# Gather matmuls of the next expert pair moved into the waits of an expert's first overflow block

## The chip, the core and the metric

The kernel runs on one NeuronCore of a Trainium2 chip. The metric is the device time of one execution in microseconds (us). Engines are named as in the profile: PE is the matmul engine (PEld its weight loads), ACT the scalar engine, DVE the vector engine, POOL the GpSimd engine, SP the engine that issues most DMAs. ACTq and SPq are DMAs that ACT and SP issue; an issue keeps its engine's instruction stream for the time shown.

## What is computed

The reference runs a two-layer trunk over 384 tokens (128 of a prompt and 256 samples) of width 1024. A layer is a token mixer (differential attention, then retention) and a mixture of 16 experts, in which each token uses two. Only the expert part matters here:

```python
s = sigmoid(t @ w_router)                    # t: 384 x 1024
gates = top-2 of 16 inside the best of 4 groups, normalised
for wg, wu, wd, ge in experts:               # wg, wu: 1024 x 512, wd: 512 x 1024
    a = silu(t @ wg) * (t @ wu) * ge[:, None]
    y = y + a @ wd
```

All of it is in float32. Which expert a token takes is known only on the chip.

## The kernel before

Both layers call `experts(l)` once on each engine; each engine has a program of its own, and semaphores order them. The 16 experts run in eight pairs. For an expert `e` (`x` is its place in the pair), PE does this:

- gate and up products of the first 64 tokens routed to the expert, lines 1089 and 1090, 8 rounds, into PSUM bank `x`;
- `overflow(e, ...)`: tokens beyond 64 are done in blocks of 32. The numbers of blocks are cumulated on the chip in a table `RT[l]`, so that an expert's blocks run from `RT[l][e]` to `RT[l][e + 1]`. PE loads both into registers (lines 998 and 999), and if they are equal it jumps over the block's code; else it loops over the blocks (`Fori`). A block gathers 32 tokens (line 1014, semaphore `o_gathered`), waits for DVE's copy (`o_rows`), transposes (1025), waits for DVE (`o_xs`), does gate and up (1031), waits for ACT's silu and DVE's product (`o_gated`), transposes (1037), waits for DVE (`o_aT`) and does the down product (1043);
- three quarters of a gather, line 986: nine products that pick, by a 0/1 matrix `sel`, the tokens of the same place in the next pair, into PSUM bank `2 + x`. It needs `sel` and `xs`, which come from the pair before;
- four transposes, line 1103, which need `gated` and signal `T`; then the last quarter of the gather (three products), then the down products, lines 1120 and 1121, which need `aT`.

A float32 product is two MATMUL records (and two weight loads) in the trace, so nine products are "x18"; a transpose is one.

ACT does for each expert: silu (line 1463), the overflow loop, and the copy that gives `aT` (line 1466, after `T`), then the copy of a finished gather half (1434). For experts before 14 the overflow loop on ACT is a silu (1442), a wait for `o_y`, and then four DMA issues that store the block's rows (line 1450). They stand ahead of line 1466 in ACT's stream:

```python
act.wait_ge(m["o_y"], o + 1)
for j in range(4):
    act.dma_start(scratch[ds(o * OVB + LAST * BLK, OVB), QC * j:QC * j + QC],
                  oy[OVB * j:OVB * j + OVB, :]).then_inc(m["o_stored"], 16)
```

`o_y` is signalled by DVE's copy of the down result (line 1935), which waits for line 1043. SP loads weights into a ring of slots: a gate or up slot is loaded again after `T` of its old expert, a down slot after `down` (line 603).

Experts 14 and 15 (`LAST` is 14) have no next pair, so no gather.

Of the kernel before, what the change touches and what calls it, by code (L numbers as in the profile page):

```python
# [16 lines left out]
P = 128  # L17
# [6 lines left out]
DEPTH = 2  # L24
# [210 lines left out]
def trunk_kernel(nc, ins, outs, scratch):  # L235
# [31 lines left out]
    with ctx:  # L267
# [30 lines left out]
        RT = [sb(f"route_tab{l}", [1, NE + 1], I32) for l in range(DEPTH)]  # L298
# [337 lines left out]
        def _(pe):  # L636
# [322 lines left out]
            def experts(l):  # L959
# [20 lines left out]

                def gather(half, kts):

                    for kt in kts:
                        out = psum[:, 2 + half, P * (kt % 4):P * (kt % 4) + P]
                        for t in range(TT):
                            last = mm(out, htok[:, t, P * kt:P * kt + P], sel[:, t].rearrange("p x s -> p (x s)"),  # L986
                                      start=t == 0, stop=t == TT - 1)
                    return last
# [7 lines left out]
                def overflow(e, wg, wu, hint):  # L996
# [3 lines left out]
                    ov = psum[:, 7, :]  # L1000
                    with unless_equal(pe, f"pe_blocks_{l}_{e}", lo, hi, hint):
# [8 lines left out]
                        with pe.Fori(lo, hi) as o:  # L1010
                            pe.wait_ge(m["o_sel"], o + e + 1)
                            for t in range(TT):
                                for j in range(4):
                                    last = mm(ov[OVB * j:OVB * j + OVB, 0:QC], osel[:, t, :], htok[:, t, QC * j:QC * j + QC],
                                              start=t == 0, stop=t == TT - 1)
                            last.then_inc(m["o_gathered"], 1)
                            if e >= LAST:
                                for t in range(TT):
                                    last = tr(psum[:, 4, P * t:P * t + P], oselw[:, t].rearrange("p n s -> p (n s)"), ident)
                                last.then_inc(m["o_selT"], 1)  # L1020
                            else:
                                pe.sem_inc(m["o_selT"], 1)
                            pe.wait_ge(m["o_rows"], o + 1)
                            for k in range(2):
                                last = tr(ov[:, QC + P * k:QC + P * k + P], osg[:, P * k:P * k + P], ident)
                            last.then_inc(m["o_turned"], 1)
                            pe.wait_ge(m["o_xs"], o + 1)
                            for kt in range(KT):
                                for j in range(4):
                                    w = (wg, wu)[j // 2]  # L1030
                                    last = mm(ov[OVB * j:OVB * j + OVB, 0:QC], ox[:, kt, :], w[kt][:, QC * (j % 2):QC * (j % 2) + QC],  # L1031
                                              start=kt == 0, stop=kt == KT - 1)
                            last.then_inc(m["o_gu"], 1)
                            pe.wait_ge(m["o_gated"], o + 1)
                            settle(pe, l)
                            for k in range(2):
                                last = tr(ov[:, BLK * k:BLK * k + BLK], oa[0:BLK, P * k:P * k + P], ident[0:BLK, 0:BLK])
                            last.then_inc(m["o_T"], 1)
                            pe.wait_ge(m["o_aT"], o + 1)
                            for k in range(4):  # L1040
                                a = oaT[:, k % 2, OVB * (k // 2):OVB * (k // 2) + OVB]
                                for j in range(4):
                                    last = mm(ov[OVB * j:OVB * j + OVB, 0:QC], a, wd[k][:, QC * j:QC * j + QC], start=k == 0, stop=k == 3)
# [1162 lines left out]
```

## Time and profile before

| | us |
|---|---|
| median of three runs | 1444.04 (1442.41 to 1446.9) |
| the profiled execution | 1440.93 |
| its span, first to last instruction | 1439.0 |
| PE busy | 1354.5 (94%) |
| DVE busy | 517.8 (36%) |
| ACT busy | 282.2 (20%) |
| mean granted PE clock | 0.983 of full speed |

The profile is of one execution. A row of a timeline has the start and the duration in us, the engine, the line, the operation, output and inputs, the count, and in brackets the idle time of that engine ahead of it with what ended it. Ends of matmuls are modelled. "issue" is idle time for which the profile shows no releaser. The expert part takes about 340 to 600 us in layer 0 and 1113 to 1410 us in layer 1.

### The profile page before, as it was taken

What the parts mean: (1) busy time and instruction counts of PE and PEld (TensorE: products, weight loads), DVE (VectorE), ACT (ScalarE), POOL (GpSimd) and SP (SyncE); (2) the same over time, 40 slices, a digit from 0 to 9 for tenths busy, and PEclk for the clock granted to TensorE, in tenths of its full rate; (3) what the DMA queues carried; (4) which work ended last, traced back from release to release, by engine and by line L of the source; (5) the groups of instructions that cost most, each with busy time, mean ns of one, the idle gap of its engine ahead of it and who ended that gap; (6) DMA issues with size and microseconds to landing.
All of it is one profiled execution on the core that took longest, in us unless ns stands there. A gap on an engine that the chain in (4) does not pass through costs nothing.

```text
span 1439.0 us, 17852 instructions
## 1 busy us (share of the span) xinstructions
PE 1354.5 (94%) x6816; PEld 768.3 (53%) x6816; DVE 517.8 (36%) x1376; ACT 282.2 (20%) x580; POOL 47.2 (3%) x63
## 2 busy tenths in 40 slices
PE   5899999997998999889999999999998998899997
PEld 2456556555444444447667567576565544444434
DVE  3145355625111111554464653744513311111123
ACT  3143344411010111231120221212111100001013
POOL 1001200000000000100000000100100000000010
PEclk9999999998999999999999999999999899999998
DMA  9967686926999999912323423224534799579891
GB/s 363 322 244 231 224 279 237 380 95 238 392 396 350 398 395 378 388 64 94 117 82 117 146 88 110 95 89 139 182 118 174 254 398 387 190 258 398 324 399 52
DMA packets 162742, 344.83 MB, mean 240 GB/s; under 512 B 5929, under 2 KB 23554, under 8 KB 162626
## 3 DMA queue, kind: packets, MB, share of 16 engines
q1 hardware_dynamic: 150320, 319.19, 60.4%
q10 hardware_dynamic: 9362, 14.37, 2.7%
q0 software_dynamic: 2944, 9.65, 2.5%
q8 instruction: 82, 1.34, 0.4%
q14 instruction: 34, 0.28, 0.1%
HBM read 324.96 MB, written 18.22 MB: 238 GB/s over the span
## 4 chain that ended last, share of the span: by engine, by line
PE 85%; DMA 6%; DVE 4%; ACT 2%; SPq 2%; issue 1%; DVEq 0%; ACTq 0%
PE psum L1089 14%; PE psum L771 11%; PE psum L786 10%; PE psum L808 9%; PE psum L1120 7%; PE psum L986 7%; PE psum L1206 5%; PE psum L937 3%; PE psum L1198 3%; DMA ring<-in_moe_w_up 3%; PE psum L673 2%; PE psum L1031 2%; DMA ring<-in_da_w_qkv 2%; SPq L569 1%; PE psum L1060 1%
## 5 line engine op out<-in xcount | busy, mean ns | idle before, releaser
L771 PE MATMUL psum<-hT,ring 128*128 128x384 f32 x512 | 173.5, 498 | 8.8 <-DMA ring<-in_da_w_qkv 5.9
L1089 PE MATMUL psum<-ring,work 128*64 128x512 f32 x384 | 170.1, 593 | 2.6 <-DMA ring<-in_moe_w_up 2.6
L1090 PE MATMUL psum<-ring,work 128*64 128x512 f32 x384 | 170.2, 594 | 0.0
L771 PEld LDWEIGHTS psum<-hT,ring 128*128 128x128 f32 x512 | 99.0, 195 | 77.4 <-issue 8.3
L808 PE MATMUL psum<-ring,hT 128*128 128x512 f32 x288 | 125.9, 593 | 0.0
L986 PE MATMUL psum<-work 128*128 128x128 f32 x768 | 106.4, 292 | 5.5 <-issue 3.5
L1089 PEld LDWEIGHTS psum<-ring,work 128*64 128x64 f32 x384 | 51.8, 137 | 111.2 <-issue 111.0
L986 PEld LDWEIGHTS psum<-work 128*128 128x128 f32 x768 | 95.0, 200 | 28.2 <-issue 24.0
L1120 PE MATMUL psum<-ring,work 128*64 128x512 f32 x192 | 89.9, 612 | 1.3 <-issue 1.2
L1975 DVE COPY work<-psum 128x512 f32<-128x512 f32 x32 | 22.1, 692 | 191.2 <-PE psum L1121 191.2
L1121 PE MATMUL psum<-ring,work 128*64 128x512 f32 x192 | 90.0, 613 | 0.0
L1969 DVE TENSOR_TENSOR work<-work,psum 64x512 f32<-64x512 f32 x32 | 22.1, 690 | 187.1 <-ACT work L1463 187.0
L808 PEld LDWEIGHTS psum<-ring,hT 128*128 128x128 f32 x288 | 54.8, 190 | 63.7 <-issue 62.1
L786 PE MATMUL psum<-ring 128*128 128x256 f32 x384 | 86.8, 379 | 0.0
L1463 ACT ACTIVATE work<-psum 64x512 f32<-64x512 f32 x32 | 18.8, 588 | 314.8 <-PE psum L1090 314.8
L786 PEld LDWEIGHTS psum<-ring 128*128 128x128 f32 x384 | 73.1, 190 | 9.8
L786 PE MATMUL psum<-ring,hT 128*128 128x256 f32 x288 | 66.1, 379 | 0.0
L2003 DVE TENSOR_TENSOR ring<-ring 128x1024 f32<-128x1024 f32 x48 | 60.8, 1283 | 2.5 <-DVE work L2012 1.3
L786 PEld LDWEIGHTS psum<-ring,hT 128*128 128x128 f32 x288 | 54.8, 190 | 12.5 <-issue 5.7
L1640 DVE SCALAR_TENSOR_TENSOR xT<-psum,mod,xT 128x128 f32<-128x128 f32 x70 | 24.7, 412 | 94.7 <-PE psum L1206 62.1
L1090 PEld LDWEIGHTS psum<-ring,work 128*64 128x64 f32 x384 | 51.9, 137 | 0.0
L1120 PEld LDWEIGHTS psum<-ring,work 128*64 128x64 f32 x192 | 24.9, 140 | 47.2 <-issue 45.0
(338 smaller groups left out, 1810.0 us busy)
## 6 DMA issues: line engine op xcount, KB each, us to landing
ring<-in_w_ada SPq DMA_DIRECT2D x24, 2048.0 KB, 12.4
ring<-in_moe_w_gate SPq DMA_DIRECT2D x24, 2048.0 KB, 13.0
ring<-in_moe_w_up SPq DMA_DIRECT2D x24, 2048.0 KB, 17.4
ring<-in_moe_w_down SPq DMA_DIRECT2D x24, 2048.0 KB, 17.9
ring<-in_da_w_qkv SPq DMA_DIRECT2D x6, 2048.0 KB, 14.8
sq<-in_moe_w_gate SPq DMA_DIRECT2D x8, 1536.0 KB, 12.3
hT<-in_moe_w_up SPq DMA_DIRECT2D x8, 1536.0 KB, 15.0
work<-in_moe_w_down SPq DMA_DIRECT2D x24, 512.0 KB, 11.3
```

What stands on the lines that cost most here:

```text
L771: last = mm(b[:, 0:TOK], w[:, kt, col:col + P], hT[:, kt, :], start=kt == 0, stop=kt == KT - 1)
L786: last = mm(b[:, 0:256], rows[k], weights[k], start=k == 0, stop=k == 3)
L808: last = mm(b, hT[:, kt, P * t:P * t + P], w[:, kt, :], start=kt == 0, stop=kt == KT - 1)
L937: last = mm(b[:, 0:TOK], w[:, h, P * (ft % 4):P * (ft % 4) + P], oT[:, h, :], start=h == 0, stop=h == HEADS - 1)
L986: last = mm(out, htok[:, t, P * kt:P * kt + P], sel[:, t].rearrange("p x s -> p (x s)"), start=t == 0, stop=t == TT - 1)
L1089: mm(psum[0:BLK, x, :], xk, wg[kt], start=kt == 0, stop=kt == KT - 1)
L1090: last = mm(psum[BLK:P, x, :], xk, wu[kt], start=kt == 0, stop=kt == KT - 1)
L1120: mm(psum[0:BLK, 5 + x, :], eaT[:, x, k, :], wd[k][:, 0:512], start=k == 0, stop=k == 3)
L1121: last = mm(psum[BLK:P, 5 + x, :], eaT[:, x, k, :], wd[k][:, 512:D], start=k == 0, stop=k == 3)
L1198: last = mm(b, a, v, start=n == 0, stop=n == len(terms) - 1)
L1206: last = mm(b[:, 0:TOK], w[:, k, P * (ft % 2):P * (ft % 2) + P], roT(k), start=k == rows[0], stop=k == rows[-1])
L2003: V.tensor_tensor(wT_[:, part], x, y, ALU.subtract).then_inc(wT_ready, 1)
```

## The change

PE's `overflow` gets the list of the nine products (empty where there is no next pair), and the waits for `sel` and `xs` now stand before it. There are three pieces of code for each expert. `more` runs the first block, by a loop from `RT[l][e]` to a new table entry `RT[l][e] + 1`, and `fill` puts three of the products behind line 1014's group, two behind the first transposes and four behind gate and up. `rest` is a second copy of the block without products, for further blocks. `none` holds the nine products alone, for experts without overflow. `none` stands behind `more` and `rest`, and the common end behind `none`. DVE writes the 16 new entries with one more small instruction, and `routed` is signalled by it.

```diff
-        RT = [sb(f"route_tab{l}", [1, NE + 1], I32) for l in range(DEPTH)]
+        RT = [sb(f"route_tab{l}", [1, 2 * NE + 1], I32) for l in range(DEPTH)]
...
+                def block_of(e, o, wg, wu, wd, fill):
...
+                    last.then_inc(m["o_gathered"], 1)
...
+                    fill(3)
+                    pe.wait_ge(m["o_rows"], o + 1)
...
+                    last.then_inc(m["o_turned"], 1)
+                    fill(2)
+                    pe.wait_ge(m["o_xs"], o + 1)
...
+                    last.then_inc(m["o_gu"], 1)
+                    fill(4)
+                    pe.wait_ge(m["o_gated"], o + 1)
...
+                    label = f"pe_blocks_{l}_{e}"
+                    pe.br_eq(lo, hi, on_true=f"{label}_none", on_false=f"{label}_more").branch_hint(hint)
+                    with nc.body(f"{label}_more", valid_engines=[pe.engine]):
...
+                        left = list(pieces)
+
+                        def fill(n):
+
+                            for kt, t in left[:n]:
+                                gather_one(kt, t)
+                            del left[:n]
+
+                        second = pe.value_load(RT[l][0:1, NE + 1 + e:NE + 2 + e], min_val=0, max_val=OVMAX + 1)
+                        end_hint = pe.mark_branch_hint_location()
+                        with pe.Fori(lo, second) as o:
+                            block_of(e, o, wg, wu, wd, fill)
+                        pe.br_eq(second, hi, on_true=f"{label}_end", on_false=f"{label}_rest").branch_hint(end_hint)
+                    with nc.body(f"{label}_rest", valid_engines=[pe.engine]):
+                        with pe.Fori(second, hi) as o:
+                            block_of(e, o, wg, wu, wd, lambda n: None)
+                        pe.br(f"{label}_end")
+                    with nc.body(f"{label}_none", valid_engines=[pe.engine]):
+                        for kt, t in pieces:
+                            gather_one(kt, t)
+                        pe.br(f"{label}_end")
+                    nc.switch_bb(f"{label}_end")
...
-                            overflow(e, wg, wu, hint)
                             more = q + 1 < NE // 2
                             if more:
                                 pe.wait_ge(m["sel"], q + 2)
                                 pe.wait_ge(m["xs"], q * 2 + x + 1)
-                                gather(x, range(4 * x, 4 * x + 3))
+                            overflow(e, wg, wu, hint, [(kt, t) for kt in range(4 * x, 4 * x + 3) for t in range(TT)] if more else [])
...
-                V.tensor_copy(RT[l][0:1, :], wm["cum"][0:1, :]).then_inc(m["routed"], 1)
+                V.tensor_copy(RT[l][0:1, 0:NE + 1], wm["cum"][0:1, :])
+                V.tensor_scalar(RT[l][0:1, NE + 1:2 * NE + 1], wm["cum"][0:1, 0:NE], 1.0, None, ALU.add).then_inc(m["routed"], 1)
```

On PE, at the first expert of layer 0, the block's code and what follows it stood like this before (lines 1014 to 1043 are the block, 986 the gather, 1103 the transposes that signal `T`):

```order
L1014 MATMUL psum<-work 32x256 [waits moe0_o_sel]
L1014 MATMUL psum<-work 32x256 x11
L1025 MATMUL psum<-base_sb,work 128x128 [waits moe0_o_rows]
L1025 MATMUL psum<-base_sb,work 128x128
L1031 MATMUL psum<-ring,work 32x256 [waits moe0_o_xs]
L1031 MATMUL psum<-ring,work 32x256 x31
L1037 MATMUL psum<-base_sb,work 128x64 [waits moe0_o_gated]
L1037 MATMUL psum<-base_sb,work 128x64
L1043 MATMUL psum<-ring,work 32x256 [waits moe0_o_aT]
L1043 MATMUL psum<-ring,work 32x256 x15
```

Now the same place has products of the gather (line 983 of the changed file) between the steps of the first block (its lines 1005, 1017, 1024, 1031 and 1037 are 1014, 1025, 1031, 1037 and 1043 of before):

```order
L1005 MATMUL psum<-work 32x256 x11
L983 MATMUL psum<-work 128x128 x3
L1017 MATMUL psum<-base_sb,work 128x128 [waits moe0_o_rows]
L1017 MATMUL psum<-base_sb,work 128x128
L983 MATMUL psum<-work 128x128 x2
L1024 MATMUL psum<-ring,work 32x256 [waits moe0_o_xs]
L1024 MATMUL psum<-ring,work 32x256 x31
L983 MATMUL psum<-work 128x128 x4
L1031 MATMUL psum<-base_sb,work 128x64 [waits moe0_o_gated]
L1031 MATMUL psum<-base_sb,work 128x64
L1037 MATMUL psum<-ring,work 32x256 [waits moe0_o_aT]
```

Nine products moved from behind the block into it. Behind the second copy of the block, PE's code for an expert without overflow follows, then the common end (line 1134 is 1103 of before):

```order
L1080 COMPARE_AND_BRANCH
L1082 UNCONDITIONAL_BRANCH
L983 MATMUL psum<-work 128x128 x9
L1086 UNCONDITIONAL_BRANCH
L1134 MATMUL psum<-base_sb,work 128x64 [waits moe0_gated]
L1134 MATMUL psum<-base_sb,work 128x64 x3
L983 MATMUL psum<-work 128x128 x3
```

An expert without overflow now jumps over two copies of the block instead of one.

## Rows read from the trace of the kernel before

**Rows 1.** The page: the gather; busy us, mean ns, idle us before it.

```profile
L986 PE MATMUL psum<-work 128*128 128x128 f32 x768 | 106.4, 292 | 5.5 <-issue 3.5
```

**Rows 2.** Source view of line 1025: ns min/median/max, first and last start.

```profile
L1025 PE MATMUL psum<-base_sb,work x14: 272/300/330, 426.6 to 1275.9; 128*128 128x128 f32 x14
```

**Rows 3.** Timeline of PE, the overflow block of expert 5, layer 0.

```profile
424.51 1.50 PE L1014 MATMUL psum<-work 128*32 128x256 f32 x24
426.62 0.44 PE L1025 MATMUL psum<-base_sb,work 128*128 128x128 f32 x2 [0.60 <-DVE work L1924]
427.57 0.41 PE L1031 MATMUL psum<-sq,work 128*32 128x256 f32 x2 [0.52 <-DVE work L1926]
...
432.28 0.30 PE L1037 MATMUL psum<-base_sb,work 64*128 64x64 f32 x2 [1.04 <-DVE work L1929]
432.96 0.64 PE L1043 MATMUL psum<-work 128*32 128x256 f32 x8 [0.38 <-DVE work L1931]
...
434.83 2.28 PE L986 MATMUL psum<-work 128*128 128x128 f32 x18
437.04 0.46 PE L1103 MATMUL psum<-base_sb,work 64*128 64x64 f32 x4
437.42 0.94 PE L986 MATMUL psum<-work 128*128 128x128 f32 x6
438.29 0.64 PE L1120 MATMUL psum<-work 128*64 128x512 f32 x1
```

**Rows 4.** Timeline of DVE, the end of the same block.

```profile
435.07 0.42 DVE L1935 COPY work<-psum 128x256 f32<-128x256 f32 x1 [2.16 <-PE psum L1043]
```

**Rows 5.** Timeline of ACT, the end of the same block.

```profile
435.69 1.86 ACTq L1450 DMA_DIRECT2D expert_rows<-work  x4
437.76 0.38 ACT L1466 ACTIVATE work<-psum 128x256 f32<-128x256 f32 x1 [6.09 <-PE psum L1103]
```

**Rows 6.** Timeline of PE, expert 1 of layer 0, without overflow.

```profile
371.08 0.46 PE L1103 MATMUL psum<-base_sb,work 64*128 64x64 f32 x4
...
372.33 0.64 PE L1120 MATMUL psum<-ring,work 128*64 128x512 f32 x1
```

**Rows 7.** Timeline of ACT, expert 1 of layer 0.

```profile
371.57 0.38 ACT L1466 ACTIVATE work<-psum 128x256 f32<-128x256 f32 x1 [2.00 <-PE psum L1103]
```

**Rows 8.** Timeline of ACT, end of the block of expert 6, layer 0.

```profile
459.91 2.90 ACTq L1450 DMA_DIRECT2D expert_rows<-work  x4
463.01 0.38 ACT L1466 ACTIVATE work<-psum 128x256 f32<-128x256 f32 x1 [7.12 <-issue]
```

**Rows 9.** Timeline of PE, behind the same block.

```profile
461.25 0.46 PE L1103 MATMUL psum<-base_sb,work 64*128 64x64 f32 x4
...
463.49 0.61 PE L1120 MATMUL psum<-ring,work 128*64 128x512 f32 x1 [0.92 <-issue]
```

**Rows 10.** Timeline of ACT, end of the block of expert 7, layer 1.

```profile
1284.77 1.79 ACTq L1450 DMA_DIRECT2D expert_rows<-work  x4
1286.74 0.38 ACT L1466 ACTIVATE work<-psum 128x256 f32<-128x256 f32 x1 [5.99 <-PE psum L1103]
```

**Rows 11.** Timeline of SP: the weight load behind `T` of expert 5.

```profile
437.59 0.37 SPq L603 DMA_DIRECT2D sq<-in_moe_w_gate  x1
```

**Rows 12.** Timeline of PE, experts 9 (layer 0) and 11 (layer 1).

```profile
504.76 0.38 PE L986 MATMUL psum<-work 128*128 128x128 f32 x2 [0.95 <-issue]
...
1343.20 1.38 PE L986 MATMUL psum<-work 128*128 128x128 f32 x10 [2.50 <-issue]
...
1344.90 1.65 PE L986 MATMUL psum<-work 128*128 128x128 f32 x6
```

**Rows 13.** A stretch: busy of PE, PEld, DVE, ACT, POOL, clock, DMA, GB/s.

```profile
1345.00:1349.00 4.00, 4.00 (x14) 2.08 (x16) 0.00 (x0) 0.98 (x2) 0.00 (x0) 0.59 1.05 388
```

**Rows 14.** The page: the queue that brings instructions; packets, MB, share.

```profile
q8 instruction: 82, 1.34, 0.4%
```

**Rows 15.** Waits, 340 to 600 us: total us, times, longest.

```profile
PE psum L1089 <- DMA ring<-in_moe_w_up: 1.7, 1, 1.7
```

More of the change, by code:

```diff
@@ L979, in experts, with gather_one @@
                     emptied(pe, ("htok", l, i))
+                def gather_one(kt, t):
+                    return mm(psum[:, 2 + kt // 4, P * (kt % 4):P * (kt % 4) + P], htok[:, t, P * kt:P * kt + P],
+                              sel[:, t].rearrange("p x s -> p (x s)"), start=t == 0, stop=t == TT - 1)
                 def gather(half, kts):
                     for kt in kts:
-                        out = psum[:, 2 + half, P * (kt % 4):P * (kt % 4) + P]
                         for t in range(TT):
-                            last = mm(out, htok[:, t, P * kt:P * kt + P], sel[:, t].rearrange("p x s -> p (x s)"),
-                                      start=t == 0, stop=t == TT - 1)
+                            last = gather_one(kt, t)
                     return last
@@ L998, in overflow @@
+                def overflow(e, wg, wu, hint, pieces):
                     lo = pe.value_load(RT[l][0:1, e:e + 1], min_val=0, max_val=OVMAX)
                     hi = pe.value_load(RT[l][0:1, e + 1:e + 2], min_val=0, max_val=OVMAX)
-                    ov = psum[:, 7, :]
-                    with unless_equal(pe, f"pe_blocks_{l}_{e}", lo, hi, hint):
+                    label = f"pe_blocks_{l}_{e}"
+                    pe.br_eq(lo, hi, on_true=f"{label}_none", on_false=f"{label}_more").branch_hint(hint)
+                    with nc.body(f"{label}_more", valid_engines=[pe.engine]):
@@ L1009, in overflow @@
                             pe.wait_ge(m["y"], e + 2)
[L1010 to L1043, printed above, removed]
-                            last.then_inc(m["o_down"], 1)
-                            if e >= LAST:
-                                pe.wait_ge(m["o_y"], o + 1)
-                                pe.wait_ge(m["o_wT"], o + 1)
-                                for k in range(2):
-                                    for j in range(4):
-                                        rows = slice(OVB * j, OVB * j + OVB)
-                                        last = mm(psum[:, OBANK[j], 0:TOK], oy[rows, P * k:P * k + P], wTo[rows, :], start=True, stop=True)
-                                    last.then_inc(m["o_comb"], 1)
-                                    pe.wait_ge(m["o_added"], o * 2 + k + 1)
-                            else:
-                                pe.sem_inc(m["o_comb"], 2)
```

41 lines of the change are left out of this document (40 added, 1 removed).

## The prediction, made blind

> **What bounds the kernel now.** The page comes first: PE is busy for 94% of the span, and the gather is one of its large groups [rows 1]. That alone says that PE's time counts, not that each part of it does. Next, how often the change acts: the transposes of line 1025 are two in a block, and there are 14 records, so seven blocks ran [rows 2]. The timelines place them in six experts (5 and 6 of layer 0; 4, 5, 6 and 7 of layer 1, where 5 has two blocks). So the products move in six places; the 22 other experts with a next pair keep their gather where it was, in other code. Third, the timeline of PE through one block [rows 3], and last the other engines at its end [rows 4, 5], since a saving on PE is worth only what the next thing to arrive allows.
>
> **The part removed from PE's row.** Behind the block the nine products fill PE from 434.83 to 437.04, 2.21 us [rows 3]. Inside the block PE idles for 0.60 us ahead of line 1025, 0.52 us ahead of 1031, 1.04 us ahead of 1037 and 0.38 us ahead of 1043 [rows 3], 2.54 us in all. Six records go into the first gap, four into the second, eight into the third. At 2.21/18 = 0.123 us each that is 0.74, 0.49 and 0.98 us against 0.60, 0.52 and 1.04. They fit but for 0.14 us in the first. Taken alone, this is worth 2.21 - 0.14 = 2.07 us an expert, 12.4 us in six: 0.9%.
>
> **What is late next.** I think nearly none of that arrives. Behind the block, PE runs line 1103 at 437.04 and could start 1120 1.25 us later, at 438.29 [rows 3]. Expert 1, with no overflow, has the same 1.25 us from 371.08 to 372.33 [rows 6], so PE is not visibly held in either. But 1120 needs `aT`, the copy of line 1466 on ACT, and ACT has the block's four DMA issues ahead of it. In expert 5 these start at 435.69, after DVE's copy of the down result (435.07 and 0.42 us) [rows 4], and take 1.86 us, to 437.55. Line 1466 starts at 437.76 and ends at 438.14; 0.15 us later PE starts 1120 [rows 3, 5]. Did 1466 wait for PE's transposes or for ACT's own issues? In expert 1 it starts 0.49 us after line 1103 [rows 6, 7]; in expert 5 it starts 0.72 us after, which is 0.21 us after the last issue. In expert 6 the issues take 2.90 us, and 1466 starts 0.20 us after them, 1.76 us after 1103, and PE idles for 0.92 us [rows 8, 9]. In expert 7 of layer 1 the gap behind the issues is 1286.74 - 1286.56 = 0.18 us [rows 10], and the three other places look alike. So in all six 1466 follows ACT's issues at once, whatever PE does. The page names "PE psum L1103" as its releaser; that is only the last semaphore, and had been there.
>
> The chain is thus line 1043, DVE 1935, four issues, 1466, 1120, and no gather is in it. Before, the gather hid it to within 0.05 us. When the gather goes, PE is through with 1103 and the last quarter 2.21 us earlier, at 438.29 - 2.21 = 436.08, and stands until about 438.24. Saved in the six: 6 x 0.05 = 0.3 us at most, not 13.3.
>
> **What is added.** (1) The chain starts at the end of the block, and the block gets longer by what does not fit: 0.14 us each, 0.8 us in six; from 0 (the modelled ends hide it) to 0.4 us each for the changes of shape. (2) `T` comes 2.2 us earlier, so SP's weight issues, now at 437.59 [rows 11], just behind ACT's, fall among them. Four issues took 1.79 to 2.90 us [rows 5, 8, 10]; the spread of 1.1 us bounds the price of each, and a gain has no reason. I take 0.1 us each, 0.6 us, since the longest came before any SP issue. (3) A third register load and the second loop's branch: PE's matmuls of 1089 and 1090 are queued ahead of them and hide them at the block's start; at its end the second branch stands where PE has 2.2 us to spare. Nothing, or up to 0.2 us each without that cover. (4) DVE's extra instruction is one row of 16 numbers before `routed`, beside the first gather: nothing. (5) Earlier `T` can start weights 2.2 us sooner. PE waits for weights once in layer 0, for 1.7 us [rows 15]; the load it waits for hangs on `T` of an expert without overflow, so I give 0 of it, and keep 1.7 us in the range.
>
> (6) The code itself, the largest term. Instructions come in 82 pieces, 1.34 MB, 16 KB each [rows 14]. A float32 product is four instructions, a transpose two, by which PE's whole old program is some 20,960, so 256 to a piece. The block is 248 and a few. A jump over it went on by one piece, which is the piece that follows anyway. Now it goes over two copies, some 540 instructions, so beyond it. Twice PE idles on "issue" in the gather of an expert without overflow, 0.95 and 2.50 us [rows 12]. I laid the programs out in pieces: these are the experts in which the jump arrives 46 and 29 instructions before the end of a piece, so that the next one is needed before it is there. I read the two as waits for code. Behind the second, PE's clock falls to half for a while: 0.59 of full speed as a mean over 4 us, and six gather records that otherwise take 0.94 take 1.65 us [rows 3, 12, 13], some 1.6 us more in all. In the new layout jumps arrive 51, 40, 32, 29 and 2 instructions before an end, and one way out of a block (expert 4, layer 1) 7 before. On the line through (46, 0.95) and (29, 2.50) the first four cost 0.5, 1.5, 2.2 and 2.5 us; for the fifth I take 3 (0 to 5), for the sixth 1, since part of it lies in the wait for ACT. With 3 us for slow clock that is 13.7 us, against 0.95 + 2.50 + 1.6 = 5.05 before: 8.7 us more. I take 7.5, as the layout is counted and not seen. Bounds: -5 (no such wait left) to +14.
>
> **The sum.** -0.3 + 0.8 + 0.6 + 7.5 = +8.6 us; rounded to +8 for what the earlier loads may give. On the profiled execution that is 1440.93 + 8 = 1449; this execution lay 3.1 us under the median of the runs, on which it is 1444.04 + 8 = 1452.
>
> **Rivals.**
> - *No gain, and code costs nothing more* (25%): the hint placed ahead of the jump has the far piece in time, and what stalls there are replace the old ones. Then +1.1 us: 1445, between 1442 and 1447. For it: 24 of the 26 jumps show no wait.
> - *Far jumps are loaded late* (13%): no jump in the old trace skips a piece, so none shows that the hint loads one further on. If each of 26 jumps waits, the price lies between 0 and the 2.50 us of [rows 12]; with matmuls queued ahead of the jump I take 0.6 us, 16 us, and 1462 (1455 to 1475). The long idle ahead of 1120, 2.2 us six times, could also pull down the clock as the 2.50 us one did, 6 x 1.6 = 10 us, which ends at the same place.
>
> The Trainium skill has a rule that speaks against this change ("Runtime: NRT & Kernel Launch", section "Instruction fetch mechanics"): prefetch is purely sequential, and a taken branch to a page outside the current two-page window waits for that page's DMA. By that rule this rival would be the case. The same section gives 16 KiB, 256 instructions, for a block, with which [rows 14] agree.
>
> - *The other side: PE's gather was what 1120 waited for* (7%). If ACT's issues got shorter, or 1466 waited for 1103 after all, PE's saving passes on: -12.4 + 0.6 = -12 us, 1432. It decides at 1466: it must start 2 us earlier against 1043. Against it: the 0.18 to 0.21 us behind the issues [rows 5, 8, 10].
> - *The old waits for code vanish* and nothing takes their place (10%): -5 + 1 = -4 us, 1440.
>
> **How the numbers follow.** Forecast 45%: no gain from the move, more waits for code, 1452 with 1446 to 1458 of its own. The rest as above. A measurement of this kernel can tell 0.3%, 4.3 us, from no change. Slower by more: most of the forecast (40%) and the 13%, 53%. Within it: 5% of the forecast, the 25% and half of the fourth rival, 35%. Faster: the 7% and half of the fourth, 12%. A range of 1438 to 1466 leaves out the 7%, and a third of the 13%, and little at the forecast's edges; where the layout is miscounted its bounds (-5, +14) are inside.
>
> **What would show it.** In the six experts: no idle left ahead of the transposes and of gate and up in the first block, but some 2 us of idle ahead of the first 1120 record (1151 in the changed file), with ACT's four issues ending 0.2 us ahead of its copy; the distance from the last record of the down group of the block to the first of 1120 stays near 3.8 us. If it falls to 1.6 us I am wrong, and the time is near 1432. In the others: idle on "issue" inside the gather or behind it, about 14 us in all, against 3.5 us before, in few experts; if it is in all, the jumps are loaded late; if in none, the time is near 1445.

## The result

The changed kernel takes 1494.18 us (median of four executions, three of them 1485.88 to 1494.38); the kernel before took 1445.24 us beside it. The fourth execution took 7960.99 us, which nothing on record explains, and the ratio leaves it out. The ratio is 1.033, interval 1.0304 to 1.0355: slower by 49 us. The forecast was 1452 with a range of 1438 to 1466, so the sign was right and the size far off.

The page of the changed kernel, first its span and the busy rows, then the queue of instructions (packets, MB, share), the chain, and the groups of the gather (983) and the down products (1151), with the idle time before them last:

```profile
span 1492.1 us, 17886 instructions
...
PE 1378.4 (92%) x6816; PEld 783.0 (52%) x6816; DVE 518.0 (35%) x1378; ACT 282.1 (19%) x580; POOL 47.3 (3%) x63
...
q8 instruction: 103, 1.69, 0.5%
...
PE 85%; DMA 4%; issue 4%; DVE 3%; SPq 2%; ACT 2%; ACTq 0%; DVEq 0%
...
L983 PE MATMUL psum<-work 128*128 128x128 f32 x768 | 113.8, 301 | 26.8 <-issue 24.8
...
L1151 PE MATMUL psum<-ring,work 128*64 128x512 f32 x192 | 97.4, 655 | 10.3 <-issue 10.2
```

PE's work is the same 768 gather records; what grew is idle time ahead of them, from 5.5 to 26.8 us [rows 1], and ahead of the down products. PE's busy time grew too, from 1354.5 to 1378.4 us, for the same number of matmuls (6816). That is slow clock: the mean granted clock fell from 0.983 to 0.967 of full speed. So of the 53.1 us between the two profiled spans some 29 us are idle time and 24 us are slow clock. 21 more pieces of code were fetched than before [rows 14]. The view of waits from 340 us on (line and releaser; us in total, times, longest) puts it more briefly:

```profile
PE psum L983 <- issue: 24.8, 8, 3.5
PE psum L1151 <- issue: 16.3, 6, 3.5
PE psum L1134 <- issue: 7.5, 3, 2.9
```

The kernel before has 3.5 us in two waits on "issue" in the gather, and none of the other two rows among its largest. So there are two losses, in different experts.

**The six experts with a block.** PE's timeline of expert 5, layer 0, in the changed kernel (start, duration, engine, line):

```profile
431.73 1.50 PE L1005 MATMUL psum<-work 128*32 128x256 f32 x24
433.16 0.94 PE L983 MATMUL psum<-work 128*128 128x128 f32 x6
433.93 0.38 PE L1017 MATMUL psum<-base_sb,work 128*128 128x128 f32 x2
434.15 0.61 PE L983 MATMUL psum<-work 128*128 128x128 f32 x4
...
438.42 1.16 PE L983 MATMUL psum<-work 128*128 128x128 f32 x8
439.53 0.31 PE L1031 MATMUL psum<-base_sb,work 64*128 64x64 f32 x2
440.22 0.64 PE L1037 MATMUL psum<-work 128*32 128x256 f32 x8 [0.38 <-DVE work L1963]
...
442.09 0.46 PE L1134 MATMUL psum<-base_sb,work 64*128 64x64 f32 x4
442.48 0.94 PE L983 MATMUL psum<-work 128*128 128x128 f32 x6
446.88 1.07 PE L1151 MATMUL psum<-work 128*64 128x512 f32 x1 [3.47 <-issue]
```

The idle times ahead of lines 1017, 1024 and 1031 are gone, filled with the moved products, and the 18 records behind the block too. From the last gate and up product to the transposes of 1134 each of the six experts became 2.13 to 2.16 us shorter, 12.9 us in all. Then PE stands: 3.47 and 2.58 us in layer 0, 2.88, 2.63, 2.13 and 2.59 us in layer 1. ACT and SP at that place:

```profile
442.95 3.23 ACTq L1481 DMA_DIRECT2D expert_rows<-work  x4
446.40 0.38 ACT L1497 ACTIVATE work<-psum 128x256 f32<-128x256 f32 x1 [7.47 <-issue]
```

```profile
442.64 0.37 SPq L603 DMA_DIRECT2D sq<-in_moe_w_gate  x1
443.06 0.54 SPq L603 DMA_DIRECT2D work<-in_moe_w_gate  x1
443.70 0.40 SPq L603 DMA_DIRECT2D hT<-in_moe_w_up  x1
444.15 4.38 SPq L603 DMA_DIRECT2D work<-in_moe_w_up  x1
```

Line 1497 (1466 before) starts 0.22 us after ACT's four issues, as it did before [rows 5, 8, 10]. The issues themselves now take 3.23, 2.36, 2.65, 2.45, 1.92 and 2.38 us, 2.50 as a mean against 2.06, with SP's issues beside them (that these are the reason is not shown by itself: the longest of the four issues of [rows 8], 1.09 us, began before SP issued anything there). After the wait the products run at half the clock; the stretch behind it in expert 5 (PE, PEld, DVE, ACT, POOL busy, then clock, DMA share, GB/s):

```profile
446.90:450.30 3.40, 3.40 (x8) 1.12 (x10) 0.00 (x0) 0.37 (x1) 0.00 (x0) 0.50 1.04 380
```

That is 3.4 us at 1.2 GHz and costs 1.7 us, in five of the six (not behind the shortest wait, 2.13 us). The account of the six: -12.9 + 15.4 (longer wait ahead of 1151) + 8.4 (clock) = +10.9 us. The distance from the last record of the block's down group to the first 1120 record (1151 now), which the prediction named as its sign, was 3.77 to 4.76 us and is 3.77 to 5.10 us: it did not fall to 1.6.

**The experts without a block.** In the two profiled executions they account for 39 us of the 53.1 us, some 37 us of it waits for code and the slow clock behind them. Expert 3 of layer 0, where the gather starts behind the jump:

```profile
403.91 2.27 PE L983 MATMUL psum<-work 128*128 128x128 f32 x18 [3.22 <-issue]
```

The views of the profile do not list branches and fetches of code; the raw records of PE's sequencer and of the queue of instructions do. For each jump, in us: time of the hint, start of the branch after the hint, how long the branch took, and the loads of code from 4 us before the hint to the end of the branch, counted from the hint.

```
changed kernel          hint     branch  took   loads of code
layer 0 expert 2       374.72   +4.90   1.51   -3.65  +3.89
layer 0 expert 3       392.81   +4.87   6.17   -0.50  +8.56
layer 0 expert 8       494.05   +5.10   6.22   +1.99  +8.95
layer 0 expert 9       512.91   +4.91   1.37   +3.82
layer 1 expert 2      1181.40   +5.12   5.54   +1.80  +8.29
kernel before
layer 0 expert 2       374.98   +4.76   0.43   +2.22
layer 0 expert 9       493.95   +4.78   0.33   none
```

Three kinds of jump are seen. Before, the target was mostly there already: 18 of the 26 taken branches took 0.33 to 0.45 us, and none more than 2.42 us. In the changed kernel only three did (0.35 to 0.47 us), since by the count of instructions most targets lie two pieces or more ahead. In 16 a load starts 3.6 to 4.6 us after the hint, the branch takes 1.1 to 2.5 us, and the matmuls queued ahead hide it. In the other 7 of the 26 no load answers the hint before the branch. The load then starts 3.2 to 4.0 us after the branch, and the branch takes 5.5 to 6.4 us. Of each, 2.8 to 3.5 us show as idle PE, 22.5 us in all, with 1.7 us of slow clock behind four.

There is a second loss in these experts. Four jumps that were not late (experts 2, 7 and 13 of layer 0, 10 of layer 1) are followed by a wait some microseconds later, inside the gather or behind it:

```profile
387.24 0.43 PE L1134 MATMUL psum<-base_sb,work 64*128 64x64 f32 x4 [2.44 <-issue]
```

The four waits are 2.44, 2.35, 2.10 and 2.84 us, 9.7 us, with slow clock behind two. Each ends 2.5 to 2.7 us after a load of the next piece of code starts. So do the two waits of the kernel before [rows 12], 2.5 us after their loads, which bears out that they were waits for code. Late jumps cost 22.5 + 4 x 1.7 = 29 us and these four 9.7 + 2 x 1.7 = 13 us, against 5 us of the second kind before: some 37 us more. A wait for weights in the last expert of layer 1 grew from 0.94 to 4.06 us beside them.

### The profile page after: what moved, and what is told of

Read it like the earlier page. It is cut to its first block, busy times and chain, and to the rows that moved or that the text cites. A ratio compares the mean times of both kernels' runs of the same rounds, so it can differ in the third digit from the quotient of the medians.

```text
span 1492.1 us, 17886 instructions
## 1 busy us (share of the span) xinstructions
PE 1378.4 (92%) x6816; PEld 783.0 (52%) x6816; DVE 518.0 (35%) x1378; ACT 282.1 (19%) x580; POOL 47.3 (3%) x63
## 4 chain that ended last, share of the span: by engine, by line
PE 85%; DMA 4%; issue 4%; DVE 3%; SPq 2%; ACT 2%; ACTq 0%; DVEq 0%
PE psum L1121 14%; PE psum L771 11%; PE psum L786 10%; PE psum L808 8%; PE psum L1151 8%; PE psum L983 7%; PE psum L1237 5%; PE psum L937 3%; PE psum L1229 3%; PE psum L673 2%; PE psum L1024 2%; DMA ring<-in_da_w_qkv 1%; DMA ring<-in_moe_w_up 1%; SPq L569 1%; PE psum L1092 1%
## 5 line engine op out<-in xcount | busy, mean ns | idle before, releaser
L1121 PE MATMUL psum<-ring,work 128*64 128x512 f32 x384 | 171.9, 598 | 4.1 <-DMA ring<-in_moe_w_up 4.1
L1122 PE MATMUL psum<-ring,work 128*64 128x512 f32 x384 | 171.9, 598 | 0.0
L983 PE MATMUL psum<-work 128*128 128x128 f32 x768 | 113.8, 301 | 26.8 <-issue 24.8
L983 PEld LDWEIGHTS psum<-work 128*128 128x128 f32 x768 | 100.8, 208 | 52.3 <-issue 48.1
L1151 PE MATMUL psum<-ring,work 128*64 128x512 f32 x192 | 97.4, 655 | 10.3 <-issue 10.2
L1152 PE MATMUL psum<-ring,work 128*64 128x512 f32 x192 | 97.8, 656 | 0.0
## 6 DMA issues: line engine op xcount, KB each, us to landing
work<-in_moe_w_down SPq DMA_DIRECT2D x24, 512.0 KB, 10.9
```

The costliest lines, as they stand in the source:

```text
L983: return mm(psum[:, 2 + kt // 4, P * (kt % 4):P * (kt % 4) + P], htok[:, t, P * kt:P * kt + P], sel[:, t].rearrange("p x s -> p (x s)"), s ...
L1121: mm(psum[0:BLK, x, :], xk, wg[kt], start=kt == 0, stop=kt == KT - 1)
L1122: last = mm(psum[BLK:P, x, :], xk, wu[kt], start=kt == 0, stop=kt == KT - 1)
L1151: mm(psum[0:BLK, 5 + x, :], eaT[:, x, k, :], wd[k][:, 0:512], start=k == 0, stop=k == 3)
L1152: last = mm(psum[BLK:P, 5 + x, :], eaT[:, x, k, :], wd[k][:, 512:D], start=k == 0, stop=k == 3)
```

## The experiments

Two theories stood at the start. **A**: ACT's four issues hand the gain of the moved products back. **C**: the jumps over a longer body cost the rest. Rival of C: the loss comes from the products inside the block or from the place of the gather, not from the length of the code.

**One part at a time.** First both loops, but the gather behind their common end for all experts, as before:

```diff
-                    pe.br_eq(lo, hi, on_true=f"{label}_none", on_false=f"{label}_more").branch_hint(hint)
+                    pe.br_eq(lo, hi, on_true=f"{label}_end", on_false=f"{label}_more").branch_hint(hint)
...
-                        left = list(pieces)
+                        left = []
...
-                    with nc.body(f"{label}_none", valid_engines=[pe.engine]):
-                        for kt, t in pieces:
-                            gather_one(kt, t)
-                        pe.br(f"{label}_end")
                     nc.switch_bb(f"{label}_end")
+                    for kt, t in pieces:
+                        gather_one(kt, t)
```

> The changed kernel's code (two copies of the block, second table entry, second branch), but no product of the gather is moved: all nine stand behind the common end, as before the change. Theory C (what costs is code: a jump over two copies lands beyond the next piece of code, and is loaded late): the experts without overflow lose what they lose in the changed kernel, about 37 us, the six with overflow 0 to 6 us; 1478 to 1488 us, and 100 or more pieces of code loaded. Rival M (the move itself costs, by waits for ACT and slow clock, and the code little): within 5 us of the kernel before, 1445.

Measured: 1456.15 us, ratio 1.0089 (1.0058 to 1.0121). The second loop alone, with nothing moved, costs 13 us. Three branches took over 5 us (layer 0 expert 12, layer 1 experts 3 and 9). That is between what the two theories gave. The length alone makes late jumps, so the rival falls as the whole cause, but it makes 3 of them and not 7. The gather's own copy behind `rest`, missing here, makes an expert's code longer still and moves all that follows; what part of the rest is due to that is not separated.

Then the products in the waits, but one loop for all blocks (a second block gathers the same again, which changes nothing in the sums):

```diff
-                        with pe.Fori(lo, second) as o:
+                        with pe.Fori(lo, hi) as o:
                             block_of(e, o, wg, wu, wd, fill)
-                        pe.br_eq(second, hi, on_true=f"{label}_end", on_false=f"{label}_rest").branch_hint(end_hint)
-                    with nc.body(f"{label}_rest", valid_engines=[pe.engine]):
...
+                        pe.br(f"{label}_end")
```

> The move alone: the products stand in the block's waits, but there is one copy of the block; where an expert has two blocks the nine products are done twice, with the same result. Experts without overflow jump over some 290 instructions instead of 540. Theory C and A (A: nothing is gained by the move, since the down products wait for ACT's copy, which stands behind four DMA issues): the six experts lose about what they lose in the changed kernel, 11 us with the slow clock, and jumps that mostly reach the next piece lose 0 to 10 us: 1456 to 1467 us. If code were no cause, about 1494, as the changed kernel. If A is wrong and the code is right: 1433.

Measured: 1455.31 us, 1.0084 (1.0051 to 1.0116). The six experts behave as in the changed kernel: -2.0 to -2.2 us each, then +1.4 to +3.0 us ahead of the down products, and slow clock in four. Two branches were over 5 us (layer 0 expert 10, layer 1 expert 14).

**ACT's issues.** The four stores of a block go behind ACT's copy for `aT` (and behind the copy of the next gather), in a loop of their own:

```diff
-                                act.wait_ge(m["o_y"], o + 1)
-                                for j in range(4):
-                                    act.dma_start(scratch[...], oy[...]).then_inc(m["o_stored"], 16)
...
                             if q + 1 < NE // 2:
                                 take_xs(q + 1, 1 - par, x)
+                            if e < LAST:
+                                store_blocks(e, lo, hi, store_hint)
```

> The changed kernel, but ACT stores an expert's overflow rows behind its copy of line 1466 and the gather's copy, not ahead of them. Theory A: line 1466 then starts some 0.5 us after PE's transposes also in the six experts, PE does not stand ahead of the down products, its clock stays up there, and the six change from +11 us against the kernel before to -13: 24 us less than the changed kernel, 1470 us. The rival (the wait of the down products is for code, or for something else on PE) expects 1494.

Measured: 1474.89 us, 1.0251 (1.0193 to 1.031; four executions, 1469.51 to 1488.44). PE and ACT at expert 5 of layer 0:

```profile
437.06 0.46 PE L1134 MATMUL psum<-base_sb,work 64*128 64x64 f32 x4
437.45 0.94 PE L983 MATMUL psum<-work 128*128 128x128 f32 x6
438.32 0.64 PE L1151 MATMUL psum<-work 128*64 128x512 f32 x1
```

```profile
437.63 0.39 ACT L1503 ACTIVATE work<-psum 128x256 f32<-128x256 f32 x1 [3.73 <-PE psum L1134]
438.42 0.60 ACT L1465 ACTIVATE work<-psum 128x512 f32<-128x512 f32 x1 [0.40 <-PE psum L983]
438.82 2.93 ACTq L1486 DMA_DIRECT2D expert_rows<-work  x4
```

The copy now follows the transposes by 0.57 us, and PE goes on without a gap. Theory A holds: 19.3 us less than the changed kernel. Five of six experts keep their 2.15 us. Seven late jumps are still there, six of them in the same experts.

The same edit in the kernel before:

> The kernel before with the same edit on ACT. Theory A: the gather behind the block covers ACT's issues but for 0.99 us in one expert and 0.37 us in another, so it gains 1 to 2 us: 1443 to 1444 us, the same within noise. If the issues held up more than that, 1435 or less; if the added branch on ACT costs in each of 28 experts, 1450.

Measured: 1446.73 us, 1.0016 (0.9994 to 1.0038). There the gather stood ahead of 1120 and hid ACT's issues; taking these away alone brings nothing. The two hid each other, so neither is worth anything while the other stands.

**The hint.** The hint for the jump goes ahead of the first gate and up product instead of the ninth, 7.4 us ahead of the branch instead of 4.9:

```diff
-                                if kt == KT // 2:
+                                if kt == 0:
                                     hint = pe.mark_branch_hint_location()
```

> The changed kernel with TensorE's hint for the jump ahead of the first gate/up product of an expert instead of ahead of the ninth, so about 9 us ahead of the branch instead of 5. Theory T (the hint comes too late for a jump that now reaches two or three pieces of code ahead): the 7 branches of 5.5 to 6.4 us go, 1460 to 1468 beside 1494. Theory N (a hint whose load falls beside the load of the next piece in sequence is lost, wherever it stands): about as many jumps are late as before, but other ones: 1480 to 1500, with at least 3 branches above 5 us, each with a load of code between 3 us before and 2.3 us behind its hint and none at 3.6 to 4.9 us behind it.

Measured: 1457.73 us, 1.0109 (1.0095 to 1.0124), 36.5 us less than the changed kernel by one moved instruction. Its waits:

```profile
PE psum L1151 <- issue: 15.6, 6, 4.0
...
PE psum L983 <- issue: 6.2, 3, 2.8
...
PE psum L1134 <- issue: 2.6, 2, 1.6
```

Line 1151 waits as before; the other two fall from 32.3 us to 8.8 us. One branch is over 5 us (layer 1 expert 3), and 23 of the 26 take 0.33 to 0.46 us. The four later waits of the changed kernel shrink as well, from 9.7 to 5.9 us. Expert 3 of layer 0 now has its hint at 386.57, loads at -3.86 and +3.73 us from it, and a branch of 0.43 us. Both theories as I had put them are half right: the late jumps go with loads of the next piece near the hint, but an earlier hint is not lost as often.

**Without the hint.**

```diff
-                    pe.br_eq(lo, hi, on_true=f"{label}_none", on_false=f"{label}_more").branch_hint(hint)
+                    pe.br_eq(lo, hi, on_true=f"{label}_none", on_false=f"{label}_more")
```

> The changed kernel without TensorE's hint for the first branch. If a branch of 5.5 to 6.4 us is one whose hint brought nothing, nearly all of the 26 taken branches now take 5.5 to 6.4 us, about 3.5 to 4.5 us of each showing: 19 more than in the changed kernel, 1494 + 19 x 4.2 = 1574, 1555 to 1595. If the long branches have another cause, the others stay at 1 to 2.5 us and the time within 10 us of 1494.

Measured: 1558.44 us (two runs), 1.0805 (1.0773 to 1.0838). 21 of the 26 branches took 5.9 to 6.7 us, the others 3.3 to 4.1 us. A row of its waits:

```profile
PE psum L983 <- issue: 71.0, 25, 3.8
```

There are 14 more branches over 5 us, and the five others take longer as well: 64 us for the 19 hints that were of use in the changed kernel, 3.4 us each. So a branch of 6 us is one whose hint brought nothing.

**Which hints are lost.** The changed kernel moved within its pieces, by met waits ahead of each layer's first expert. (The text on record says 64 instructions; an instruction holds two waits, so it was 32, two times.)

```diff
+                for _ in range(64):
+                    pe.wait_ge(m["sel"], 1)
                 pe.wait_ge(m["routed"], 1)
```

> The changed kernel with 64 instructions more on TensorE's sequencer ahead of the first expert of each layer (waits that are met already), so that all that follows stands 64 instructions further within its pieces of code and nothing else differs. If the late jumps hang on where hint and branch stand within a piece, another set of experts is late, and the number of branches above 5 us differs from 7 in 26: anything from 2 to 10, the time 1494 plus about 4.2 us for each one more and minus as much for each one less, 1473 to 1507. If the doubled loop costs a fixed amount by its length alone, it stays within 1490 to 1498, with the same experts late.

Measured: 1492.46 us, 1.033 (1.031 to 1.0349). The total is the same, the experts are not: eight branches over 5 us, in experts 4, 9, 10 of layer 0 and 2, 3, 9, 13, 14 of layer 1, of which two were late in the changed kernel. The time alone would have spoken for a fixed cost of length; the branches speak for place and moment. Over the four kernels with two loops and the hint at the ninth product there are 25 such branches. In 22 of them a load of the next piece starts between 0.6 us before and 3.0 us after the hint; in three none does. Seven other taken jumps with such a load were not as late. So the two go together, but it is no full rule.

The times of the loads say more. In the kernels with the early hint (the one above and three further down) 17 hints have a load of code from 1.3 us before to 1.4 us after them and another after that; the second never starts sooner than 5.7 us after the first. In layer 0 expert 7 of the kernel with both cures they start at +1.08 and +6.89 us, with the branch at +7.62 us, and the branch takes 1.68 us. A hint 4.9 us ahead of the branch, with a load between 0.5 us before and 3.0 us after it, would by that distance get its own load 5.2 to 8.7 us after it, behind the branch; one 7.4 us ahead still gets it in time if the other load starts less than 1.7 us after it. A jump between the two fits: layer 0 expert 3 in the kernel with later stores has loads at -0.58 and +5.41 us, the branch at +5.10, and it takes 2.79 us. The other six of the seven fit less well: there the second load starts 3.2 to 5.0 us after the first, so the distance is not fixed. Even so, in the 22 cases the hint may have been late rather than lost. No run changed this distance alone, so that is an explanation that fits the records and not one that is shown.

**With one loop and the later stores**, which should have kept the gain:

> Nine gather products inside the waits of the block, but one loop for all blocks of an expert, and ScalarE's four scratch stores of a block issued behind its copy that gives aT. In the run with one loop alone each of the six experts with a block was 2.1 us shorter up to its transposes and then lost 1.4 to 3.0 us ahead of its down products and up to 1.7 us to a slow clock behind that. Theory (ScalarE's issues are what hands the gain back): those six losses go, the six gains of 2.1 us stay, 12.9 us in all; jumps over one loop cost 0 to 8 us more than before, since two of 26 were late in the run with one loop. 1434 to 1441 beside 1444 of before. Rival (the gain cannot be had, since the gating chain and not the products sets the end of the block): 1447 or more.

Measured: 1441.29 us, 0.9995 (0.9982 to 1.0008). My theory said 1434 to 1441, and the interval says no change. No expert waits ahead of its down products any more, and four of the six have their -2.15 us (5 and 6 of layer 0, 4 and 7 of layer 1). The rest went elsewhere: layer 0 expert 10 +3.0 and layer 1 expert 14 +2.3 us (the two late jumps, as in the first kernel with one loop), layer 1 expert 1 +2.6 us, and expert 5 +5.2 instead of -2.2 us, where PE stands 4.04 us inside the first products of a block and goes on 2.6 us after a load of code starts.

With the early hint too:

> The kernel with one loop, the nine products in its waits and ScalarE's stores behind the copy, and the hint ahead of the first gate/up product instead of the ninth. Theory T: no branch above 2.5 us, 1431 to 1436. Theory N: 0 to 3 branches above 5 us, 1432 to 1444, not told apart from the same kernel with the later hint.

Measured: 1440.58 us, 0.9991 (0.9971 to 1.001). The same two branches are late, so here the hint's place does not decide.

Then an attempt to move all hints away from the starts of pieces, in the kernel with one loop and the later stores, by lengthening each expert's code (and by 120 instructions of the same kind ahead of the routing of layer 1, not shown here):

```diff
                     last.then_inc(m["o_T"], 1)
+                    for _ in range(64):
+                        pe.wait_ge(m["sel"], 1)
                     pe.wait_ge(m["o_aT"], o + 1)
```

> The kernel with one loop, the nine products in its waits and the later stores, and 64 met waits (32 instructions) in TensorE's wait for the block's aT, so that an expert's code is 506 instructions long instead of 474 and all hints but the first stand 42 to 138 instructions into a piece of 256, none near a piece's start; 120 instructions more ahead of the second layer's routing. In the kernel with one loop the two late jumps (layer 0 expert 10, layer 1 expert 14) had their hints 20 and 1 instructions into a piece. If the place in the piece decides, no branch takes above 3 us and the time is 1424 to 1433; the 32 instructions of a block cost up to 1 us each on seven blocks where the wait doesn't hide them. If the losses hang on timing more than on place, 1 to 4 branches above 5 us, 1434 to 1448.

Measured: 1475.66 us, 1.0232 (1.0207 to 1.0257). No branch took more than 2.57 us, as place would have it. But the filling cost far more than I had allowed: a block grew by 3 to 5 us for 32 instructions, and the 120 instructions ahead of the routing of layer 1 cost 8.7 us. The right test puts them where they are jumped over, behind the loop in the bodies of experts that have no block on this input:

```diff
                         with pe.Fori(lo, hi) as o:
                             block_of(e, o, wg, wu, wd, fill)
+                        for _ in range({(0, 7): 8, (0, 8): 6, (0, 9): 6, (1, 8): 8, (1, 9): 8, (1, 10): 8, (1, 11): 8, (1, 12): 6}.get((l, e), 0)):
+                            pe.wait_ge(m["sel"], 1)
```

> The kernel with one loop, the nine products in its waits and ScalarE's stores behind the copy for aT, plus 10 (layer 0) and 19 (layer 1) instructions in the bodies of experts that have no block, behind their loop, so that they are jumped over and never run. They move layer 0 expert 10 and layer 1 expert 14, whose jumps were late in all three kernels with this code, 10 and 29 instructions on, to a place in the piece of 256 where layer 0 expert 3 was in time. If place decides: neither is late, 5.3 us less than the same kernel without them, 1434 to 1438. If something else decides (what runs beside them on other queues): both stay late, 1440 to 1443.

Measured: 1441.43 us, 0.9989 (0.9974 to 1.0004). The two late jumps are gone (2.2 and 1.9 us, hidden), by 10 and 29 instructions of shift: place decides those two. The time did not follow. PE's first record of expert 15, layer 0, in this kernel:

```profile
579.62 1.08 PE L1117 MATMUL psum<-ring,work 128*64 128x512 f32 x1 [5.22 <-DMA ring<-in_moe_w_up]
```

Before, it stood at 580.42, after a wait of 1.70 us for the same DMA [rows 15]. PE comes 4.3 us earlier and starts 0.8 us earlier. The stretch up to there, for this kernel and then the kernel before:

```profile
300.00:580.00 280.00, 264.29 (x1566) 131.47 (x1566) 58.80 (x172) 31.58 (x59) 5.74 (x6) 0.97 0.93 348
```

```profile
300.00:580.00 280.00, 262.56 (x1564) 131.44 (x1562) 57.45 (x167) 31.45 (x59) 4.46 (x5) 0.98 0.91 341
```

With the DMA engines 91 to 93% busy, what PE saves in layer 0 turns into a wait for weights at its end. In layer 1 expert 5 still stands for code, and expert 6 keeps only a part of its gain behind the expert with two blocks (in the kernel with one loop and later stores, ACT's new loop sits there for 5.6 us between its first and second round; no record says for what).

> The same with the hint ahead of the first gate/up product. With place deciding and the hint early no taken branch is above 3 us: 1432 to 1438, faster than the kernel before by 0.3 to 0.7 per cent. If the early hint only swaps which loads come late: within 0.3 per cent of the kernel before.

Measured: 1441.54 us, 1.0001 (0.9988 to 1.0015). No late jump either; the wait for weights at the end of layer 0 is 4.1 us (1.7 us before).

**Both cures in the changed kernel**, and the hint alone in the kernel before:

> The changed kernel, both loops in it, with the two cures together: ScalarE's scratch stores behind its copy for aT, and TensorE's hint ahead of the first gate/up product. If the two causes are separate they add up: 1494 less 20 for the stores and less 36 for the hint gives 1438, 1433 to 1443, the six gains of 2.1 us kept and at most two branches above 5 us. If both cures act on the same loss (the late jumps, since a late jump also shifts ScalarE's work), the second brings less: 1450 or more.

Measured: 1441.37 us, 0.999 (0.9974 to 1.0006). From 1494 the stores took 19 us and the hint 36.5 us away, and both together 53, so they are separate causes and account for the whole 49 us. The 12.9 us of the moved products should have come on top, and do not: the profile still has one late jump (3.2 us idle), 1.0 to 3.2 us behind four others, and 2.9 us inside the block of expert 6, layer 1. The rows that had 26.8 and 10.3 us:

```profile
L983 PE MATMUL psum<-work 128*128 128x128 f32 x768 | 111.9, 298 | 10.1 <-issue 8.1
...
L1151 PE MATMUL psum<-ring,work 128*64 128x512 f32 x192 | 92.5, 627 | 0.2
```

> The kernel before with the hint ahead of the first gate/up product. Its jumps reach one piece ahead, 22 of its 26 taken branches already take under 0.5 us or are hidden by PE's queue of work: no change, 1440 to 1447. Were the waits for code in it a matter of the hint too, it would lose some 5 us: 1437 to 1440.

Measured: 1444.9 us, 1.0013 (0.9998 to 1.0028): nothing, as it had no late jump to lose.

No version here is faster than the kernel before by more than can be told.

## Why the prediction was half right

- *The part removed, 2.07 us an expert*: 2.13 to 2.16 us measured, in all six. The products fit, and the 0.14 us of term (1) is some 0.06.
- *What is late next*: right. The gather hid ACT's four issues; nothing of the 12.9 us arrived, and with the issues moved it did in five of the six experts (-19.3 us against the changed kernel, with the slow clock).
- *Step (2), SP's issues beside ACT's, 0.1 us each*: mis-sized. The mean of the four issues rose by 0.44 us, 2.6 us in six, inside the bound of 1.1 us each. It matches the 15.4 - 12.9 = 2.5 us.
- *The slow clock behind the wait for ACT*: I had it at 6 x 1.6 us, but as a side remark to a rival of 13%, and left it out of the sum. It came five times at 1.7 us, 8.4 us. It followed from my own forecast of 2.2 us idle, and belonged in the sum. These last two are most of the 10.9 us where the sum had 1.1.
- *Step (6), the code, 7.5 us, bounds -5 to +14*: this failed; it was 37 us. I priced only the pieces behind a jump's landing, by two waits of the old trace, and took the jump itself as free wherever no piece boundary was near. The part that I priced came out nearly as I had it: four such waits with their slow clock, 13 us, for 13.7 (in four places and not six, so that the sum is closer than its terms). The part that I left out, the jump itself, cost the other 29 us. The row I lacked is a jump over more than one piece, and the nearest bound was not 2.50 us but what a branch costs with no load under way: 5.5 to 6.4 us. The rival "far jumps are loaded late" had the mechanism, with 0.6 us on each of 26. It was 7 of 26, 2.8 to 3.5 us idle each and 4.2 us as a mean with the slow clock. My sign for it, idle in few experts or in all, was too coarse as well: it came in few experts, as I had said of my own forecast, but with 24.8 us on "issue" ahead of 983 and 7.5 us ahead of 1134 in place of 14 us in all.
- *Step (5), earlier weights, 0*: nothing was gained, as I had it, but a wait for weights in layer 1 grew by 3.1 us, for which the sum had no term. And the 1.7 us wait of [rows 15] was more than a detail. It says that layer 0 ends on the weights. The other side's 1432 leaves that out: in the kernel with the jumped-over instructions PE came there 4.3 us earlier, and 0.8 us of it arrived.

The rule that I set against the change (the Trainium skill, "Runtime: NRT & Kernel Launch", section "Instruction fetch mechanics") says that a taken branch out of the two-page window waits for its page. The runs bear that out for a jump over both loops without a hint, 5.9 to 6.7 us in 21 of 26. With a hint in time such a jump took 0.33 to 0.46 us in 23 of 26 cases in the kernel with the early hint, which the rule leaves out.

What stays open: why a hint is lost. A load of the next piece near it goes with it in 22 of 25 cases, and a shift of the code by 10 to 32 instructions changes which ones. That the hint's own load then comes too late fits the times of the loads, but no run tests it by itself; what the sequencer does in the other three is not shown. Open too is what makes a piece of code late inside a block (expert 5 of layer 1) in the kernels with one loop.

## What to carry over

When work is taken out from behind a wait, look at what that work was hiding on the other engines; here each of two things hid the other, and only with both away did the six experts become shorter. Code that is jumped over has a length, and once a jump goes past the next piece all its cost hangs on one hint: put the hint as early as it will go, and count branches above 5 us, which show nowhere on the page but as "issue". A wait has a second price in the slow clock behind it: 24 of the 53 us here. And before a saving on one engine is priced for a stage, look for the last wait of that stage: a short wait for weights at its end can cap what is saved ahead of it.

## What was not expected of the hardware

- In the changed kernel a piece of code is loaded 3.6 to 4.6 us after the hint that asks for it, or 3.2 to 4.0 us after a branch that had no use of one; the branch then takes 5.5 to 6.4 us (up to 6.7 us without hints). A jump to a piece that is there takes 0.33 to 0.47 us. A wait for a piece ends 2.5 to 2.7 us after its load starts.
- A hint can bring nothing at all: 25 times in four kernels, 22 of them with a load of the next piece starting from 0.5 us before to 3.0 us after it.
- A wait of 2.1 to 3.5 us on PE was followed, five times in six, by 3.4 us at half the clock (0.50 granted), a loss of 1.7 us.
- An already met pair of waits costs PE's sequencer some 0.07 to 0.1 us when it runs: 8.7 us for 120 of them, and 3.2 us later at the first expert for 32.
